# Convolution over even and odd positions, and modulation products in four column groups

## The reference, cut to what matters

```python
mod = jax.nn.silu(c) @ w_ada[l] + b_ada[l]            # 1 x 6144
sh_m, sc_m, gt_m, sh_f, sc_f, gt_f = jnp.split(mod, 6, axis=-1)
h = rms_norm(x, g_pre_mix[l]) * (1.0 + sc_m) + sh_m
z = h @ w_in[l]
v = z_val * jax.nn.sigmoid(z_gate)                    # 2048 x 512
y[t, ch] = sum over k of conv_w[k, ch] * v[t - 30 + k, ch] + conv_b[ch]
a_out = silu(layer_norm(y) * ln_g + ln_b)
b_out = s5_layer(z_ssm, ...)
o = concatenate([rms_norm(a_out), rms_norm(b_out)]) @ w_out[l]
x = x + gt_m * rms_norm(o, g_post_mix[l])
h = rms_norm(x, g_pre_ffn[l]) * (1.0 + sc_f) + sh_f
x = x + gt_f * rms_norm(moe_ffn(h, ...), g_post_ffn[l])
```

## Time and profile before

| what | value |
|---|---|
| time, median of 3 runs | 2880.58 us (2875.21 to 2881.06) |
| profiled execution, its own time | 2885.38 us |
| its span | 2883.7 us |
| TensorE busy | 2631.2 us |
| VectorE busy | 1573.5 us |
| ScalarE busy | 1147.0 us |
| GpSimd busy | 1472.3 us |

### The profile page before, as it was taken

How to read it: one execution, slowest core, us unless ns; L and a number is a source line. 1 busy time by engine, 2 the same in 40 slices (tenths; PEclk the granted TensorE clock), 3 DMA queues, 4 the chain that set the end, 5 groups by cost and what they waited for, 6 DMA issues and landing times.

```text
span 2883.7 us, 49464 instructions
## 1 busy us (share of the span) xinstructions
PE 2631.2 (91%) x11395; PEld 1894.4 (66%) x11396; DVE 1573.5 (55%) x2558; ACT 1147.0 (40%) x1534; POOL 1472.3 (51%) x1756
## 2 busy tenths in 40 slices
PE   6999998997999997599999999999999999999980
PEld 2755663523566665388878878888778877777760
DVE  6379977992666666233444433354455544454435
ACT  4133212223322232234444444454555555555432
POOL 2012206115566665145555556557777777766756
PEclk8999999997899998799999999999999999999995
DMA  8152505454322221557777778888889988889877
GB/s 267 62 119 73 203 1 84 177 177 139 136 80 98 102 93 55 195 144 196 195 201 212 199 193 230 225 222 243 253 263 277 286 264 256 247 259 267 243 210 269
DMA packets 305610, 534.62 MB, mean 185 GB/s; under 512 B 39254, under 2 KB 205142, under 8 KB 304778
## 3 DMA queue, kind: packets, MB, share of 16 engines
q1 hardware_dynamic: 251770, 355.93, 37.3%
q0 software_dynamic: 51472, 173.70, 25.4%
q10 hardware_dynamic: 2304, 4.20, 0.4%
HBM read 395.76 MB, written 138.01 MB: 185 GB/s over the span
## 4 chain that ended last, share of the span: by engine, by line
PE 36%; issue 17%; POOL 10%; POOLq 6%; DVE 2%; ACT 0%; DMA 0%; SPq 0%; DVEq 0%
PE psm L1100 27%; PE psm L1046 5%; POOL arena L2153 2%; PE psm L1093 2%; POOL arena L2150 2%; POOL st L2143 2%; POOLq L2149 2%; POOLq L2171 1%; POOLq L2170 1%; POOLq L2162 1%; POOL arena L2163 1%; POOL st L2027 1%; PE psm L1068 1%; PE psm L1122 1%; POOL st L2026 1%
## 5 line engine op out<-in xcount | busy, mean ns | idle before, releaser
L1100 PE MATMUL psm<-whi,xhi 128*128 (+1 forms) x1424 | 577.0, 405 | 43.2 <-DVE hlo L1915 16.9
L1100 PE MATMUL psm<-whi,xlo 128*128 (+1 forms) x1424 | 559.1, 393 | 0.0
L1100 PE MATMUL psm<-wlo,xhi 128*128 (+1 forms) x1424 | 557.9, 392 | 0.0
L1909 DVE TENSOR_TENSOR arena<-psm,arena 128x256 f32<-128x256 f32 x178 | 75.6, 424 | 631.5 <-ACT arena L1452 627.8
L2158 POOL TENSOR_TENSOR wlo<-raw,whi (+1 forms) x64 | 330.5, 5164 | 42.5 <-ACT whi L1481 42.5
L1100 PEld LDWEIGHTS psm<-whi,xhi 128*128 128x128 f32 x1424 | 269.3, 189 | 115.8 <-issue 45.4
L1756 DVE SCALAR_TENSOR_TENSOR arena<-arena,cw 128x1024 f32<-128x1024 f32 x240 | 336.0, 1400 | 8.6
L1100 PE MATMUL psm<-whi,hhi 128*128 (+1 forms) x712 | 298.3, 419 | 44.3 <-issue 22.9
L2167 POOL DMA_INDIRECT acc_d<-arena x162 | 279.2, 1724 | 57.5 <-issue 52.6
L1100 PEld LDWEIGHTS psm<-whi,xlo 128*128 128x128 f32 x1424 | 269.1, 189 | 58.2
L1100 PEld LDWEIGHTS psm<-wlo,xhi 128*128 128x128 f32 x1424 | 269.8, 189 | 51.3
(11 more groups left out here) (353 smaller groups left out, 3993.1 us busy)
## 6 DMA issues: line engine op xcount, KB each, us to landing
raw<-in_we_gate_dram SPq DMA_DIRECT2D x64, 1024.0 KB, 8.3
raw<-in_we_up_dram SPq DMA_DIRECT2D x64, 1024.0 KB
raw<-in_we_down_dram SPq DMA_DIRECT2D x64, 1024.0 KB, 5.1
arena<-in_w_ada_dram SPq DMA_DIRECT2D x12, 2048.0 KB
arena<-in_x_dram SPq DMA_DIRECT2D x32, 512.0 KB, 5.5
h_d<-arena SPq DMA_DIRECT2D x17, 512.0 KB, 2.6
acc_d<-arena SPq DMA_DIRECT2D x17, 512.0 KB, 4.8
arena<-in_w_in_dram SPq DMA_DIRECT2D x16, 512.0 KB, 6.1
```

The costliest lines, as they stand in the source:

```text
L1100: m = TE.matmul(o, a, w, start=(n == 0), stop=(n == len(todo) - 1))
L1909: tt(htmp, psm[:, bank, 0:DE], sigb, ALU.mult).then_inc(s_hm_ready, 1)
```

## The change

The convolution is computed from even and odd positions. `v` is stored by parity: `v[:, q, 0]` and `v[:, q, 1]`, 528 positions each with 15 of history; ScalarE reads PSUM with step 2 to write it. With three filters of half length, `ca` (even taps on even positions), `cb` (odd taps on odd positions) and `cc` (sums of neighbouring taps, `cws`, on the sum of both, `both`), the even outputs are ca + cb, and the odd ones cc less ca one position on, less cb. A tile has 3 tensor_scalar and 44 scalar_tensor_tensor over 512 or 513 elements, the sum `both` over 527, and three joins. The three filters are advanced in turn, each waiting only for its own last step.

A modulation product is spread over four column groups: silu(c) is in `c32`, which has 32 columns a piece of which the first holds it and the others zeros, and piece k goes to PSUM rows 32 (k mod 4) and on. ScalarE copies all 128 rows (`fours`), TensorE adds them by a product with a column of ones (`ada_sum`), and ScalarE copies the row. Products 4 to 7 stay behind glu(1); 8 to 11 are put behind turns 0 to 3 of the last norm, and the last sum behind turn 4. ScalarE's scaling of w_out comes behind its part of products 4 to 7. At the start of the kernel the weights of product 3 are loaded ahead of x tiles 4 to 7. SyncE loads product n ahead of the store of n-4. VectorE takes all eight statistics of the last norm ahead of the row products. The first mixed half-tile is taken in turns 6 and 8.

```diff
@@ -39,6 +39,8 @@
...
 CH = TPH
 NC = HT // CH
...
         csig = sb("csig", [P, KD])
...
+        cws = work[:, 3712:3776].rearrange("p (q j) -> p q j", q=CT)
...
@@ -413,9 +422,10 @@
...
-        segs = [bofl[0:1, 0:512], bofl[0:1, 512:1024], ytok[0:1, :], ly[0:1, :]] + \
+        segs = [tabs[0:1, 2048:2560], tabs[0:1, 2560:3072], ytok[0:1, :], ly[0:1, :]] + \
                [work[0:1, n * 512:(n + 1) * 512] for n in range(2)] * 4
-        biasr = [tabs[0:1, n * 512:(n + 1) * 512] for n in range(4)] + [eg[0:1, 4096 + n * 512:4608 + n * 512] for n in range(4)] * 2
+        fours = [bofl[:, (n % 2) * 512:(n % 2 + 1) * 512] if n < NADA else stage[n % 2] for n in range(12)]
+        biasr = [tabs[0:1, n * 512:(n + 1) * 512] for n in range(4)] + [xbr[0:1, n * 512:(n + 1) * 512] for n in range(4)] * 2
...
@@ -442,6 +452,13 @@
...
+        def v_half(q, b):
+
+            return v[:, q, :, HP + b * 256:HP + (b + 1) * 256]
+
+        def by_parity(a):
+            return a.rearrange("p (i o) -> p o i", o=2)
...
@@ -549,7 +566,7 @@
...
-                sp.wait_ge(s_dva_free, DVA["ada", n] + 1)
+                sp.wait_ge(s_dva_free, DVA["sum", n] + 1)
...
@@ -565,9 +582,9 @@
...
                 load_x(n)
             load_ada(2)
+            load_ada(3)
             for n in range(XG, TPH):
                 load_x(n)
-            load_ada(3)
...
@@ -680,10 +697,10 @@
...
             for n in range(8, 12):
                 sp.wait_ge(s_dv_full, DVN["ada", n - 4] + 1)
-                store_mod(n - 4)
                 if n == 8:
                     sp.wait_ge(s_mm_full, MMN["glu", 1, 1, 3] + 1)
                 load_ada(n)
+                store_mod(n - 4)
...
@@ -853,8 +870,14 @@
                 b = take_dv(("ada", n))
                 pe.wait_ge([s_ada_in0, s_ada_in1, s_ada_in2, s_ada_in3][n % 4], 32 * (n // 4 + 1))
                 for k in range(KD):
-                    TE.matmul(b[0:1, :], ccol[:, k:k + 1], wada[n][:, k, :], start=(k == 0), stop=False)
-                TE.matmul(b[0:1, :], one[0:1, :], biasr[n], start=False, stop=True).then_inc(s_dv_full, 1)
+                    o = b[32 * (k % 4):32 * (k % 4 + 1), :]
+                    TE.matmul(o, c32[:, k, :], wada[n][:, k, :], start=(k < 4), stop=(k >= 5))
+                TE.matmul(b[0:32, :], ident[0:1, 0:32], biasr[n], start=False, stop=True).then_inc(s_dv_full, 1)
+
+            def ada_sum(n):
+                b = take_dv(("sum", n))
+                pe.wait_ge(s_dva_free, DVA["ada", n] + 1)
+                TE.matmul(b[0:1, :], one[:, :], fours[n], start=True, stop=True).then_inc(s_dv_full, 1)
 
...
@@ -868,8 +891,10 @@
             m.then_inc(s_dv_full, 1)
             for n in range(1, NADA):
                 ada(n)
+                ada_sum(n - 1)
...
@@ -1022,8 +1047,10 @@
...
-            for n in range(NADA, 12):
+            ada(4)
+            for n in range(5, 8):
                 ada(n)
+                ada_sum(n - 1)
 
...
@@ -1134,13 +1161,18 @@
...
             for i in range(TPH + 2):
                 norm_turn(1, i)
+                if i < 4:
+                    ada(8 + i)
+                    ada_sum(7 + i)
                 if i == 4:
+                    ada_sum(11)
+                if i == 6:
                     pe.wait_ge(s_mm_free, len(mmk))
                     pe.wait_ge(s_dv_free, len(DVV))
                     pe.wait_ge(s_dva_free, len(DVA))
                     pe.wait_ge(s_wout_ready, KD)
                     mix_half(0, 0, [0])
-                if i == 6:
+                if i == 8:
                     mix_half(0, 0, [1])
...
@@ -1237,6 +1269,11 @@
...
                 act.wait_ge(s_dv_full, b + 1)
+                SC.copy(fours[n], dv[b % 4]).then_inc(s_dva_free, 1)
+
+            def ada_sum(n):
+                b = DVN["sum", n]
+                act.wait_ge(s_dv_full, b + 1)
                 if n >= NADA + 2:
...
@@ -1292,10 +1329,11 @@
...
             ada(0)
             row_stats(0, psm[:, 0:2, :].rearrange("p a n -> p (a n)"))
-            ada(1)
-            ada(2)
+            for n in range(1, NADA):
+                ada(n)
+                ada_sum(n - 1)
+            ada_sum(NADA - 1)
             row_stats(1, psm[:, 0:2, :].rearrange("p a n -> p (a n)"))
...
@@ -1388,12 +1426,14 @@
...
+            ada(4)
+            for n in range(5, 8):
+                ada(n)
+                ada_sum(n - 1)
             act.wait_ge(s_small_in, 16 * NSMALL)
             act.wait_ge(s_wout_in, 16 * KD)
             for k in range(KD):
                 SC.activation(wout[:, k, :], wout[:, k, :], ACT.Copy, scale=gout[:, k:k + 1]).then_inc(s_wout_ready, 1)
-            for n in range(NADA, 12):
-                ada(n)
 
             def square_mix(i):
...
@@ -1500,6 +1540,11 @@
...
             for i in range(TPH + 2):
                 norm_turn(1, i)
+                if i < 4:
+                    ada(8 + i)
+                    ada_sum(7 + i)
+                if i == 4:
+                    ada_sum(11)
                 if i == 5:
...
@@ -1577,8 +1622,9 @@
...
+            do(V.memset(c32[:, :, :], 0.0))
             dve.wait_ge(s_csig_ok, 1)
-            V.tensor_mul(ccol[:, :], ccol[:, :], csig[:, :]).then_inc(s_csig_ok, 1)
+            V.tensor_mul(c32[:, :, 0], ccol[:, :], csig[:, :]).then_inc(s_csig_ok, 1)
...
@@ -1748,25 +1796,49 @@
...
                 for q in range(CT):
                     dve.wait_ge(s_v_ready, (h * CT + q + 1) * 2)
-                    o = cacc[:, q, :]
-                    do(ts(o, v[:, q, 0:HT], cw[:, q, 0:1], col[:, 0, q:q + 1], ALU.mult, ALU.add))
-                    for k in range(1, TAPS):
-                        m = stt(o, v[:, q, k:k + HT], cw[:, q, k:k + 1], o, ALU.mult, ALU.add)
-                        if k < TAPS - 1:
-                            do(m)
-                        else:
-                            m.then_inc(s_conv_ready, 1)
+                    even, odd = v[:, q, 0], v[:, q, 1]
+                    both = cacc[:, q, 0:VH - 1]
+                    ca, cb, cc = ((cacc[:, 1, 0:n + 1], cacc[:, 2, 0:n], cacc[:, 2, n:]),
+                                  (cacc[:, 2, 0:n + 1], cacc[:, 3, 0:n], cacc[:, 3, n:]),
+                                  (cacc[:, 3, 0:n + 1], v[:, 0, 0, HP:HP + n], v[:, 0, 1, HP:HP + n]),
+                                  (v[:, 0, 0, HP:HP + n + 1], v[:, 0, 1, HP:HP + n], v[:, 1, 0, HP:HP + n]))[q]
+                    if q:
+                        dve.wait_ge(s_conv_ready, h * CT + q)
+                        sync()
+                    do(tt(both, odd[:, 0:VH - 1], even[:, 1:VH], ALU.add))
+                    done = {}
+                    for j in range(HK):
+                        for key, o, x, w in (("a", ca, even[:, j:j + n + 1], cw[:, q, 2 * j:2 * j + 1]),
+                                             ("b", cb, odd[:, j:j + n], None if j == HK - 1 else cw[:, q, 2 * j + 1:2 * j + 2]),
+                                             ("c", cc, both[:, j:j + n], cws[:, q, j:j + 1])):
+                            if w is None:
+                                continue
+                            if j:
+                                dve.wait_ge(s_dve_step, done[key])
+                                done[key] = add(stt(o, x, w, o, ALU.mult, ALU.add))
+                            else:
+                                done[key] = add(ts(o, x, w, None, ALU.mult))
+                    sync()
+                    bias = col[:, 0, q:q + 1]
+                    y = cacc[:, q, :].rearrange("p (i o) -> p o i", o=2)
+                    do(stt(cc, cc, bias, ca[:, 1:n + 1], ALU.add, ALU.subtract))
+                    add(stt(y[:, 0], ca[:, 0:n], bias, cb, ALU.add, ALU.add))
+                    tt(y[:, 1], cc, cb, ALU.subtract).then_inc(s_conv_ready, 1)
                     if h == 0:
                         dve.wait_ge(s_conv_ready, q + 1)
-                        V.tensor_copy(v[:, q, 0:PAD], v[:, q, HT:HT + PAD]).then_inc(s_v_tail, 1)
+                        if q == CT - 1:
+                            sync()
+                            do(V.memset(v[:, 0, 0, VH - 1:VH], 0.0))
+                        V.tensor_copy(v[:, q, :, 0:HP], v[:, q, :, n:n + HP]).then_inc(s_v_tail, 1)
 
             states(0)
             conv(0)
             states(1)
             conv(1)
-            for k in range(TPH, TPH + 5):
+            for k in range(TPH, 2 * TPH):
                 norm_stats(k)
 
 
@@ -1775,8 +1847,6 @@
             do(tt(row[0], row[0], rtmp[:, 0], ALU.mult), stt(row[1], row[1], 1.0, rtmp[:, 1], ALU.add, ALU.mult),
                tt(row[3], row[3], rtmp[:, 2], ALU.mult), V.memset(selcum[:, 0, :], 0.0), V.memset(ones64, 1.0))
             V.tensor_copy(ndt[:, 3:4], ndt[:, 0:1]).then_inc(s_row_ready, 1)
-            for k in range(TPH + 5, 2 * TPH):
-                norm_stats(k)
             dve.wait_ge(s_wr_in, 32)
 
             def choose(i):
```

More of the change, by code:

```diff
@@ L41 @@
 PAD = TAPS - 1
+HP, HK = PAD // 2, (TAPS + 1) // 2
+VH = HT // 2 + HP + 1
 CH = TPH
@@ L58 @@
```

(56 more changed lines are left out.)

## The result

The changed kernel takes 2935.15 us (median of 4 runs, 2913.61 to 2944.94) against 2880.79 for the kernel before: ratio 1.0165, 95% interval 1.0126 to 1.0203. It is slower by 1.65%, where 2852 us had been forecast. Its profiled execution took 2933.41 us for a span of 2931.2, 47.5 more than before.

What follows compares the result with a forecast made beforehand. TensorE's products and VectorE's convolution were taken to bind the last norm's start together. Mixing resuming 29.9 us earlier, +0.5 at the start and +0.5 for strided reads gave -28.9 us: 2852 us from 2880.58, range 2843 to 2869.

Steps and rivals of the forecast that it cites:

- Convolution: VectorE's convolution of half 1: 31.1 us a tile, 139.5 in all including 15.1 lost beside GpSimd, ending at 615.6, not 652.95.
- A stall in half 1 from the strided reads: Sign that would prove the forecast wrong: half 1 stalling because ScalarE reads PSUM with step 2; no size given.
- Two engines reach the norm together, and 703.31 arrives at the end: TensorE (659.3) and VectorE (653.0) both gate the last norm; any shift of mixing's resumption at 703.31 reaches the end time.
- Passes 0.60 us apart: VectorE's new convolution: passes over 512 elements start 0.60 us apart, 47 making 28.2 us a tile.
- Products in four groups, 1.74 + 0.95: TensorE's modulation products: 16 instructions in 1.74 us plus 0.95 for the bias, 2.7 a product where it was 7.90.
- Two groups at a time, 3.5: Rival for TensorE's products: only two column groups run together, 3.5 + 0.95 us a product, 2859 us in all; chance 0.22.
- w_out without cover: ScalarE before the last norm: w_out scaling, moved behind the products, adds 8.4 us, putting the first norm copy at 619.0.
- Four products between the turns hidden: Last norm: TensorE's first four turns take 4.8 us with a product each, nearly hidden by GpSimd's 4.59.
- SyncE's list: Last norm: the first mixed tile is issued 10.4 us behind the copy of the last product's sum, at 649.5.
- third product waits for the first store: Last norm: GpSimd's third product waits for the first output store, issued 0.4 us behind the mixed tile, landed 2.2 later, 652.1.
- Half clock in the norm: Rival for TensorE in the last norm: products 5.4 us, sums 1.8, turns 9.5; 15 us gained, 2866 us; chance 0.10.
- Start of the kernel, strided reads: +0.5 each: Kernel start with reordered weight loads: net +0.5 us (-1.5 to +2.6); ScalarE's step-2 PSUM reads: +0.5 us, up to +3.

Runs made afterwards that it cites:

- e1: Changed kernel with the first convolution pass of each round of three waiting for the pass directly before it: 2888.44 us, ratio 1.0002 to the kernel before.
- e6: Changed kernel with GpSimd's gate product done on only 8 of its 512 elements: 2939.45 us in one run (kernel before, same chip: 2883.14).
- e10: Kernel before's convolution, with new four-column-group products all ahead of the last norm: 2889.74 us, ratio 1.0016 to the kernel before.
- e11: Kernel before's products in their old place, with the new convolution and a gap each round: 2886.78 us, ratio 1.0018 to the kernel before.
- e4: As e1, with all eight products behind glu(1) ahead of the last norm and w_out scaled ahead of them: 2869.77 us, ratio 0.9923 to the kernel before.
- e5: As e1, with SyncE's first norm stores and first mixed tile moved ahead of the row broadcasts: 2876.55 us, ratio 0.9976 to the kernel before.
- e8: Changed kernel with every convolution pass waiting for the one directly before it: 2901.52 us, ratio 1.007 to the kernel before.
- e9: As e4, but a gap only each fifth round and one w_out scaling behind each product's copies: 2867.46 us, ratio 0.9944 to the kernel before.
- e7: Changed kernel with a gap in the convolution passes every fifth round only: 2889.12 us in one run (kernel before, same chip: 2883.14).

## Why the prediction was wrong, point by point

**The step that failed** stands under *Convolution*: "15.1 us are lost while GpSimd works beside; I keep them", with "The convolution of half 0 becomes as much shorter and yields nothing". Both treat GpSimd's interference as a tax on VectorE. The row that I had the earlier trace rows was of passes drained one by one, where GpSimd gets a turn in each gap and VectorE pays. The change removes the gaps, and I priced them at their worth to VectorE alone. In their place the runs showed that the payer changes: GpSimd, where it comes to a chain that neither a gap nor GpSimd itself has broken for some 4 us, waits to its end, up to 27 us, and TensorE is late by 31.5 us in half 0 and another 33.3 in half 1. One gap a round (e1) takes all of it away, and 8 elements instead of 512 (e6) take 7 of the 64.8. No rival covered it. "A stall in half 1 from the strided reads" named a stall, but for a wrong reason.

Of the miss at the resumption (748.2 against a forecast 673.4, 74.8 us), 64.8 are those stalls. The other 10 lie in the last norm.

- *Two engines reach the norm together, and 703.31 arrives at the end.* Right: e10, e11 and e4 above. Resumptions of +19.5, +44.9 and +63.9 us gave 1.0072, 1.0165 and 1.0221, that is 21, 48 and 64 us. The other timed runs came out 6 to 16 us above what their resumptions give (e1 6, e4 7, e11 8, e5 11, e8 13, e9 14, e10 16). A part of that lies in the one trace of the kernel before: its half 1 starts at 392.10, that of e1, e4, e5, e8 and e10 between 385.75 and 387.50. Counted from there to the resumption, e1 and e4 differ from it by 0 and -22.7 us, and the timed runs say +1 and -22. e10 and e9 still come out 10 and 14 us above, more than their intervals allow. Why stays open; the stage of routed experts varies by as much (below).
- *Passes 0.60 us apart.* The step is 0.66: 188 passes make 11.3 us. VectorE's own gain is real: conv(1) took 145.5 us (507.35 to 652.9) against a forecast of 139.5 and 176.9 before, but it began 31 us late.
- *Products in four groups, 1.74 + 0.95.* Right: 660.92 to 662.77 is 1.85, with the bias 2.83. Two groups at a time, 3.5, is refuted, and the 2.2 estimated was too long; the granted clock was 1.00 from 661 to 668 us. In the norm, at a granted clock of 0.50 (689.5 to 693.1), one takes 3.57 (689.54 to 693.11).
- *w_out without cover.* Right: the first norm copy comes 22.8 us behind glu(1), forecast 22.9; only its place moved.
- *Four products between the turns hidden; SyncE's list; third product waits for the first store.* The mechanism was right, the size was not. From first copy to resumption 54.4 us were forecast and 64.5 measured. The last sum was copied 23.7 us behind the first norm copy instead of 20.1 (the granted clock was 0.50 from 684 to 700 us, so the rival *Half clock in the norm* came true for part of the way), the mixed tile's issue followed 10.8 later (10.4), and the third product stood 6.9 behind that issue (725.15), where I had a landing time of 2.6. Against the 43.3 of before, that is a loss of 21 us, which the forecast charged as 11. With the stalls gone but these terms true (e1) the change is worth nothing: the first norm copy comes 10 us later than forecast, since conv(1) ends 12 later, and the norm is 14 longer (68.7).
- *Start of the kernel, strided reads: +0.5 each.* The first turn is at 60.54 instead of 60.85; a strided copy takes 583 ns, as before. Both nothing.

## What to carry to other kernels

Before making a VectorE chain tighter, look at which GpSimd operations run beside it and who waits for them: the drains that look like waste may be the other engine's turns. Leave a gap at intervals that the waiting side can bear; here one in 2 us cost 0.13 us and one in 10 us did as well (e7, a single run, and e9 beside e4). Work moved into a stage that another list paces should be costed to the end of that list, and where two engines bind together, both edits must be judged as one.

## What was not expected of the hardware

Back-to-back passes with two SBUF inputs, starting 0.66 us apart, kept GpSimd out for 14.7, 23.0 and 27.0 us, to the end of the chain rather than of one instruction, even operations of 8 elements (up to 20.2 us) and of one (15.1). A single wait on the directly preceding pass, 0.13 us, let it in. Operations that came at most 3.44 us behind a gap or behind GpSimd's own last one were let in without a gap, those that came 4.54 us or more behind were not. When both are at work with gaps, the cost falls on VectorE (0.75 becomes 1.47 to 1.64 us). The same stage of routed experts, untouched by any edit, took 1974 to 1989 us from the start of the first to the start of the last `whi` by `xhi` product in the profiled executions (1978 in the kernel before, 1980 in the changed one). The intervals of ten runs, 0.3 to 0.4% to either side, are of the same size; that this stage makes them is not shown.
